# Attention heads' loop with the next pair's first transpose moved ahead of the last pair's second values, together with three smaller edits of the same kernel

## The reference

```python
# first block, layer 1: attention over compressed, selected and windowed keys
# 16 heads of 64, in 4 groups of keys; with T = 256 each branch sees the whole sequence
s_cmp = einsum('btghd,bcgd->bghtc', q, k_cmp);  p_cmp = masked_softmax(s_cmp, ...)
o_cmp = einsum('bghtc,bcgd->btghd', p_cmp, v_cmp)
s_sel = einsum('bqghd,bgqmd->bghqm', qb, ks);   p_sel = masked_softmax(s_sel, ...)
o_sel = einsum('bghqm,bgqmd->bqghd', p_sel, vs)
s_w = einsum('bqghd,bkgd->bghqk', qb, kw);      p_w = masked_softmax(s_w, mask_w)
o_win = einsum('bghqk,bkgd->bqghd', p_w, vw)
o = gb[..., 0:1] * ocb + gb[..., 1:2] * o_sel + gb[..., 2:3] * o_win
y = o.reshape(B, T, 1024) @ w_out               # b_w_out

# first block, both layers: feed-forward, 4096 wide
y = jnp.square(jax.nn.relu(h @ ff_w_in[layer])) @ ff_w_out[layer]

# second block: feed-forward with a 3x3 depthwise convolution, 2816 wide
u, gate = jnp.split(h @ w_up, 2, axis=-1)
u = dwconv_grid(u, w_cf, b_cf, rows, width)
y = (jax.nn.silu(u) * gate) @ w_down
x = x + gt2 * rmsnorm(y, g_post_ffn)
```

## Time and profile before

| | |
|---|---|
| median of 3 runs | 1033.72 us |
| the profiled execution, its own time | 1034.27 us |
| its span | 1032.5 us |
| PE, weight loads (PEld), DVE, ACT busy | 97%, 85%, 77%, 52% of the span |
| granted TensorE clock, mean | 0.998 |

### The profile page before, as it was taken

One profiled execution on the slowest core, in us unless ns is written; L12 is line 12 of the kernel. 1 busy time (PEld: TensorE's weight loads), 2 busy tenths in 40 slices (PEclk: granted clock), 3 DMA queues, 4 the chain that ended last, 5 costly groups with the idle time before them and its releaser, 6 DMA issues.

```text
span 1032.5 us, 17024 instructions
## 1 busy us (share of the span) xinstructions
PE 1005.6 (97%) x6953; PEld 882.6 (85%) x6953; DVE 798.3 (77%) x1196; ACT 537.9 (52%) x706; POOL 76.2 (7%) x80
## 2 busy tenths in 40 slices
PE   6999999999999999999999999999999999999996
PEld 3687799888888999887989899898998789999995
DVE  2458798777988987867968778872796889878896
ACT  4353644445446457765545444455764565454543
POOL 0000000000000000000720000000890000000000
PEclk9999999999999999999999999999999999999999
DMA  9998699887997998003988787724344185656501
GB/s 340 387 391 334 232 339 360 310 333 263 357 327 258 287 369 317 2 2 124 391 305 322 260 289 281 245 78 136 124 163 160 46 285 205 199 169 203 167 39 42
DMA packets 130333, 243.62 MB, mean 236 GB/s; under 512 B 6586, under 2 KB 95311, under 8 KB 124111
## 3 DMA queue, kind: packets, MB, share of 16 engines
q1 hardware_dynamic: 125616, 238.77, 65.7%
q10 hardware_dynamic: 4639, 3.76, 1.3%
HBM read 239.37 MB, written 1.05 MB: 233 GB/s over the span
## 4 chain that ended last, share of the span: by engine, by line
PE 74%; DVE 11%; DMA 5%; SPq 3%; ACT 3%; issue 3%; DVEq 0%; ACTq 0%
PE bank L1959 21%; PE bank L1891 12%; PE bank L1893 12%; PE bank L1892 12%; DVE wlo L1174 3%; DMA raw<-in_a_w_in_dram 3%; SPq L635 2%; PE bank L1971 2%; PE bank L2244 1%; DMA raw<-in_b_w_in_dram 1%; PE bank L1847 1%; PE bank L1797 1%; PE bank L2270 1%; DMA raw<-in_ff_w_in_dram 1%; ACT whi L705 1%
## 5 line engine op out<-in xcount | busy, mean ns | idle before, releaser
L1174 DVE TENSOR_TENSOR wlo<-raw,whi 128x2048 fp32r<-128x2048 f32 x144 | 330.9, 2304 | 51.6 <-ACT whi L705 50.6
L705 ACT ACTIVATE whi<-raw 128x2048 fp32r<-128x2048 f32 x144 | 274.1, 1904 | 146.2 <-PE bank L1959 80.4
L1891 PE MATMUL bank<-hcat,whi 128*128 128x256 f32 x1096 | 312.5, 285 | 1.1 <-DVE wlo L1174 1.1
L1893 PE MATMUL bank<-hcat,wlo 128*128 128x256 f32 x1096 | 309.9, 283 | 0.0
L1892 PE MATMUL bank<-hcat,whi 128*128 128x256 f32 x1096 | 309.9, 283 | 0.0
L1891 PEld LDWEIGHTS bank<-hcat,whi 128*128 128x128 f32 x1096 | 209.8, 191 | 7.7 <-issue 3.0
L1892 PEld LDWEIGHTS bank<-hcat,whi 128*128 128x128 f32 x1096 | 209.9, 192 | 1.5
L1893 PEld LDWEIGHTS bank<-hcat,wlo 128*128 128x128 f32 x1096 | 209.9, 192 | 0.0
L1755 DVE SCALAR_TENSOR_TENSOR cvt<-ut,vec,cvt 128x189 f32<-128x189 f32 (+2 forms) x176 | 68.1, 429 | 21.0 <-ACT cvt L1137 18.6
L1959 PE MATMUL bank<-whi,fhi 128*128 128x512 f32 x240 | 76.5, 400 | 0.0
L1959 PE MATMUL bank<-whi,flo 128*128 128x512 f32 x240 | 75.4, 395 | 0.0
(11 more groups left out here) (425 smaller groups left out, 1651.1 us busy)
## 6 DMA issues: line engine op xcount, KB each, us to landing
raw<-in_ada_w_dram SPq DMA_DIRECT2D x40, 1024.0 KB, 8.3
raw<-in_ff_w_in_dram SPq DMA_DIRECT2D x32, 1024.0 KB, 7.2
raw<-in_ff_w_out_dram SPq DMA_DIRECT2D x32, 1024.0 KB, 6.9
raw<-in_w_ada_dram SPq DMA_DIRECT2D x24, 1024.0 KB, 6.2
raw<-in_w_up_dram SPq DMA_DIRECT2D x22, 1024.0 KB, 5.0
raw<-in_w_in_dram SPq DMA_DIRECT2D x12, 1024.0 KB, 5.4
raw<-in_w_down_dram SPq DMA_DIRECT2D x11, 1024.0 KB, 4.9
raw<-in_ada_w_dram SPq DMA_DIRECT2D x16, 512.0 KB, 12.2
```

What stands on the lines that cost most here:

```text
L705: act.activation(whi[:, m % SPL, 0:w], raw[:, pl.nm[m] % RAW, 0:w], ACT.Copy).then_inc(s_hi, 1)
L1174: dve.tensor_tensor(wlo[:, m % SPL, 0:w], raw[:, pl.nm[m] % RAW, 0:w], whi[:, m % SPL, 0:w], ALU.subtract).then_inc(s_lo, 1)
L1891: pe.matmul(dst, wh[:, kt, n], ah[:, kt, :], start=kt == 0, stop=False)
L1893: mm = pe.matmul(dst, wl[:, kt, n], ah[:, kt, :], start=False, stop=kt == KT - 1)
```

## The change

- In the heads' loop `turn(2p)` now stands ahead of `values(2p-1)`.
- In the last iteration only token tile 0 of `M_BO[0]` stands before `turn(15)`; tile 1 stands between `values(14)` and `values(15)`.
- `oP` is now the first address behind the tiles that stay whose distance from `whi` is a multiple of 512: 193664 in place of 193536. All tiles of the region move up by 128 bytes.
- In `conv_epi` of the last chunk, the `wlo` between the taps is gone. Its first half stands behind the taps, ahead of `fa`, and its second half between `fa` and `clo`.

```diff
@@ -263,6 +263,7 @@
     raw = sb("raw", [P, RAW, CH])
+    whi_at = at[0]
     whi = sb("whi", [P, SPL, CH], F32R)
@@ -308,7 +309,7 @@
     rsy = sb("rsy", [P, 2])
-    oP = place(at[0], 512)
+    oP = whi_at + (at[0] - whi_at + 511) // 512 * 512
     LIMIT = 229368
@@ -1173,6 +1174,12 @@
+            def lo_half(m, i):
+                if i == 0:
+                    dve.wait_ge(s_hi, m + 1)
+                n = slice(1024 * i, 1024 * i + 1024)
+                return dve.tensor_tensor(wlo[:, m % SPL, n], raw[:, pl.nm[m] % RAW, n], whi[:, m % SPL, n], ALU.subtract)
@@ -1756,17 +1763,22 @@
-                        if n == 3:
-                            splits((M_UP[c + 1] if c + 1 < CF else M_DN[c]) + 1)
+                        if n == 3 and c + 1 < CF:
+                            splits(M_UP[c + 1] + 1)
                     if c + 1 < CF:
                         splits(M_GA[c + 1] + 1)
+                    else:
+                        lo_half(M_DN[c], 0)
                     dve.wait_ge(s_mm, M_GA[c] + 1)
                     dve.wait_ge(s_sil, c + 1)
                     if c:
                         dve.wait_ge(s_cact, c)
                     dve.tensor_tensor(fa[:, :, :], sl[:, :, :], ps[4 + c % 2][:, :].rearrange("p (k t) -> p k t", t=T), ALU.mult)\
                        .then_inc(s_fa, 1)
-                    splits(M_DN[c] + 1)
+                    if c + 1 < CF:
+                        splits(M_DN[c] + 1)
+                    else:
+                        lo_half(M_DN[c], 1).then_inc(s_lo, 1)
@@ -2291,15 +2303,16 @@
                 for p in range(NPAIR):
+                    turn(2 * p)
                     if p:
                         values(2 * p - 1)
-                    turn(2 * p)
                     if p + 1 < NPAIR:
                         scores(p + 1)
                     else:
 
                         pe.wait_ge(s_Sev, NH)
-                        rows_onto_y(M_BO[0], *h_rows(0), first=True)
+                        split_ready(M_BO[0])
+                        tile_onto_y(M_BO[0], *h_rows(0), 0, True)
                     turn(2 * p + 1)
...
                     values(2 * p)
+                tile_onto_y(M_BO[0], *h_rows(0), 1, True).then_inc(s_mm, 1)
                 values(NH - 1)
```

## The result

The changed kernel took 1053.05 us, the median of four runs (1050.74 to 1056.92), against 1034.44 us for the kernel before on the same chip: a ratio of 1.0186, with a 95% interval from 1.016 to 1.0212. The forecast was 1039.9 us, with a range up to 1045. The direction was right and the size was not: 18.6 us more in place of some 6. The profiled execution took 1052.53 us, with a span of 1050.8. Lines of PE's functions now stand 12 further down, those of ACT 1, and those of DVE 7 in the heads' loop (1 at `wlo`, 12 at `clo`).

A forecast was written before the change was run, and what follows sets the result against it. PE, without slack in the heads' loop, was taken as the bound. 1034.27 + 12.3 (loop) - 0.56 (`o_tm` wait) - 1.3 (tail) - 4.3 (region) = 1040.4 us, 1039.9 for the median; range 1037.4 to 1045.

The forecast's parts named there:

- What bounds the kernel: Whole span: PE is busy for 97%, in the heads' loop for all of it, and its delays pass to the end.
- The ring: Heads' loop: turn, values, gated and branches, scores out, exponentials, turn; 8.92 us a pair in place of 7.11, costing 12.3 us.
- third rival: Heads' loop: PE standing still drops its clock to 1.2 GHz, turn and values double, 17 us more, 1057; chance 0.04.
- The wait for `o_tm`: End of the loop: splitting `M_BO[0]` removes PE's wait, gaining 0.56 us, bounds 0 and 0.7.
- The tail: Last chunk's `conv_epi`: moving `wlo` in halves ends `clo` 1.45 us earlier, of which 1.3 us can be had.
- The region: Output matmuls: stationary tiles moved off multiples of 512 bytes save 0.10 us in each of 43 groups, 4.3 us; bounds 0 and 5.8.
- The rival that it does nothing: Output matmuls: the region's place changes nothing, so the time is 1044.2 us; chance 0.22.
- The sum: Whole kernel: 1034.27 + 12.3 - 0.56 - 1.3 - 4.3 = 1040.4 us, taken as 1039.9 for the median; chance 0.66.

The follow-up runs named there:

- e_warm: The changed kernel with 24 small matmuls of zeros added ahead of the moved turn in pairs 1 to 7; 1040.65 us, ratio 1.0061.
- e_no_turn: The changed kernel with the heads' loop back in the old order, the other edits kept; 1029.87 us, ratio 0.9957 against the kernel before.
- e_turn: The kernel before with only the loop's order changed, `turn(2p)` ahead of `values(2p-1)`; 1057.33 us, ratio 1.0221.
- e_idle: The kernel before, same order, but a pair's first turn also waits for the second head's exponentials, from pair 1 on; 1046.26 us, ratio 1.0114.
- e_region: The kernel before with only the region's place changed, `oP` 193664 in place of 193536; 1030.42 us, ratio 0.9974.
- e_ring_short: The changed kernel with `branches(p-1)` on DVE moved behind `scores_out(2p+2)`; 1045.69 us, ratio 1.01 against the kernel before.

## Why the prediction was wrong

- **What bounds the kernel** was right: PE had no slack in the loop, and each delay of it passed to the end.
- **The ring** was right, with its place and its links. The forecast had 8.92 us for a pair, and at full clock it is 8.81; the rows show the joins 0.1 shorter. At full clock the loop's loss, read in e_warm against e_no_turn up to the load ahead of `M_BO[1]`, is 11.2 us (473.31 against 462.10), 11.5 with the 0.33 that e_warm was ahead at the first group of the feed-forward. The forecast was 12.3, bounds 11.3 to 13.
- **The step that failed** is the third rival, "PE's clock falls", and the sentence that set it aside: "the granted clock stays at 1.00 in a stretch in which PE is busy for 3.62 of 5 us". That is one stretch of 5 us, with one wait among matmuls of 512 columns. It doesn't show what seven waits of 1.0 to 2.1 us in a row do in work of small matmuls. e_turn shows that the moved turn needs neither the split nor the region for it, e_idle that waits of about 1 us alone bring the clock down, in the old order too, and e_warm that it stays up when they are filled but for 0.63 to 0.74 us. The loop was near it before: three of nine executions without the waits have one dip each. The rival got a chance of 0.04, and the clock cost more than all the waiting (12.6 us against 11.5).
- **Its price**, had it been believed, was 17 us "in six pairs". The runs show 12.6: 7.9 in the ring, where the clock is down for a part of the time only, and 4.7 behind the ring, which the forecast didn't think of.
- **The wait for `o_tm`**: gone, as forecast, but worth 0.19 and not 0.56. What the split costs PE was counted at nothing, and 0.37 of the 0.56 is lost again. The split puts one more change from 512 columns to transposes or values, and back, into the work; that this is the 0.37 was not isolated.
- **The tail**: 1.3 forecast, 1.31 measured.
- **The region**: 4.3 forecast from 43 groups of 0.10. The groups did go from 5.58 to 5.47, but e_region gives 2.7 us by the ratio (1.7 to 3.7) and 3.8 in the trace. The rival that it does nothing is refuted in the trace. The reason given was half right: it is not the address of the stationary tile by itself, but how it lies against the moving one. The page of the Trainium skill that spoke against it, "SBUF — State Buffer", section "SBUF: two separate sides", has no row for this, and the measurement decides.
- **The sum**, with sizes read in the traces: 11.5 + 12.6 - 0.2 - 1.3 - 3.8 = 18.8, against 18.3 in the profiled executions (1052.53 less 1034.27) and 18.6 in the medians.

## What to carry to other kernels

Where PE has no slack and the change makes it wait often, price the wait twice: once as time, and once as time at the lower clock in the work around it and behind it; one calm stretch elsewhere in the trace doesn't exclude that, and the mean clocks of several executions of the kernel before can show that it is near already. Before moving an instruction ahead, walk the ring that it closes through the other engines' written orders: that sum was right within 0.1 us a pair. And place tiles on purpose: a stationary tile like the moving one within 512 bytes, and the DMA target `raw` at a multiple of 512, gave 0.7% together with no change of the work.

## What the runs showed of the hardware that was not expected

- In the loop, from 404 to 460 us, the mean granted clock was 0.82 where PE stood still for 1.0 to 2.1 us in each pair (the changed kernel), 0.85 with about 1.2 us (e_ring_short), 0.91 with 0.84 to 1.04 us (e_idle), and 1.00 with 0.63 to 0.74 us (e_warm).
- It fell there without any standing still too: once in each of three executions of nine, by 1.6 us of the time (0.79 from 436 to 444 us in e_region, PE busy for 8.00 of 8).
- It stayed low behind the standstills: 0.50 for all of 469 to 479 us in the changed kernel, with PE busy throughout.
- Matmuls of zeros in bf16, whose results nobody reads, kept it up: 24 of them, 1.3 us in a pair, gave back 12.4 us.
- A group of 24 matmuls of 512 columns takes 5.47 or 5.58 us by how the stationary and the moving tile lie against each other within 512 bytes (or 256, which the five places don't part).
- Loads into `raw` ran at 410 in place of 390 GB/s when it, `x` and `hcat` started at a multiple of 512 and not 128 above one.
